# Mixer weights split once: parts kept in DRAM and loaded into the operands' ring in later blocks

## The reference

```python
z = h @ w_in                      # q, k, v, g, a_low, conv's b/c/h, cross-attention's query
o = gla_chunked(q, k, v, log_a)   # gated linear attention, 4 heads
y_gla = rms_norm(o) * silu(g)
y_conv = c_b * causal_short_conv(c_c * c_h, conv_w)
y_xa = memory_cross_attention(xq, mk, mv)           # into 256 memory tokens
mix = concatenate([y_gla, y_conv, y_xa]) @ w_out
x = layer_norm(alpha * x + mix)
ff = square(relu(x @ w_ff1)) @ w_ff2
x = layer_norm(alpha * x + ff)
```

## Time and profile before

| | us |
|---|---|
| median of 3 runs (2060.28 to 2061.87) | 2060.31 |
| the profiled execution, its own time | 2059.97 |
| its span, first to last instruction | 2058.2 |
| PE busy | 2042.5 (99%) |
| DVE busy | 1424.0 (69%) |
| ACT busy | 976.8 (47%) |
| POOL busy | 223.6 (11%) |

### The profile page before, as it was taken

One profiled execution on the slowest core, in us unless ns is written; L12 is line 12 of the kernel. 1 busy time (PEld: TensorE's weight loads), 2 busy tenths in 40 slices (PEclk: granted clock), 3 DMA queues, 4 the chain that ended last, 5 costly groups with the idle time before them and its releaser, 6 DMA issues. The chain is left out here.

```text
span 2058.2 us, 29111 instructions
## 1 busy us (share of the span) xinstructions
PE 2042.5 (99%) x11424; PEld 1679.4 (82%) x11424; DVE 1424.0 (69%) x2131; ACT 976.8 (47%) x1323; POOL 223.6 (11%) x391
## 2 busy tenths in 40 slices
PE   9999999999999999999999999999999999999998
PEld 8778788778777878888888888888888888888887
DVE  6687668756866688766757776766656668766477
ACT  5454544455445447655546544545433334433333
POOL 3000000000000003245301121111100000000000
PEclk9999999999999999999999999999999999999999
DMA  6143252425142525367566787776977657756664
GB/s 188 53 122 116 70 167 60 134 62 170 57 123 62 175 68 168 126 227 217 190 225 209 251 315 265 271 279 236 339 245 267 194 193 230 241 195 194 193 219 162
DMA packets 244329, 374.36 MB, mean 182 GB/s; under 512 B 18032, under 2 KB 119504, under 8 KB 244192
## 3 DMA queue, kind: packets, MB, share of 16 engines
q1 hardware_dynamic: 213536, 275.82, 41.4%
q0 software_dynamic: 30656, 96.67, 13.9%
HBM read 272.81 MB, written 99.61 MB: 181 GB/s over the span
## 5 line engine op out<-in xcount | busy, mean ns | idle before, releaser
L1781 DVE TENSOR_TENSOR w_lo<-w_b,w_hi 128x1024 fp32r<-128x1024 f32 x142 | 173.6, 1224 | 154.3 <-ACT w_hi L1748 154.0
L1748 ACT ACTIVATE w_hi<-raw 128x1024 fp32r<-128x1024 f32 x142 | 150.1, 1059 | 232.3 <-PE main L71 98.3
L1781 DVE TENSOR_TENSOR w_lo<-raw,w_hi 128x1024 fp32r<-128x1024 f32 x142 | 173.7, 1224 | 111.4 <-ACT w_hi L1748 111.2
L1748 ACT ACTIVATE w_hi<-w_b 128x1024 fp32r<-128x1024 f32 x142 | 150.0, 1057 | 157.5 <-PE aux L71 79.7
L69 PE MATMUL main<-xT_lo,w_hi 128*128 128x512 f32 x512 | 210.4, 411 | 0.0
L71 PE MATMUL main<-xT_hi,w_hi 128*128 128x512 f32 x512 | 200.1, 391 | 0.0
L70 PE MATMUL main<-xT_hi,w_lo 128*128 128x512 f32 x512 | 199.7, 390 | 0.0
L1137 DVE TENSOR_TENSOR w_lo<-raw,w_hi 128x1024 fp32r<-128x1024 f32 x114 | 138.8, 1221 | 70.9 <-ACT w_hi L811 69.2
L69 PE MATMUL main<-x_lo,w_hi 128*128 128x512 f32 x448 | 174.3, 389 | 0.2 <-ACT z L2092 0.2
L69 PE MATMUL sc<-x_lo,w_hi 128*128 128x512 f32 x448 | 174.3, 389 | 0.2 <-ACT z L2092 0.2
L70 PE MATMUL sc<-x_hi,w_lo 128*128 128x512 f32 x448 | 174.3, 389 | 0.0
(11 more groups left out here) (306 smaller groups left out, 4499.4 us busy)
## 6 DMA issues: line engine op xcount, KB each, us to landing
raw<-in_w_in_dram SPq DMA_DIRECT2D x80, 512.0 KB, 3.9
h_dram<-z SPq DMA_DIRECT2D x64, 512.0 KB, 4.0
raw<-h_dram SPq DMA_DIRECT2D x112, 256.0 KB, 2.7
w_b<-h_dram SPq DMA_DIRECT2D x112, 256.0 KB, 2.8
h_dram<-h_s SPq DMA_DIRECT2D x48, 512.0 KB, 4.0
raw<-in_w_out_dram SPq DMA_DIRECT2D x32, 512.0 KB, 3.5
raw<-in_w_ff_dram SPq DMA_DIRECT2D x32, 512.0 KB, 6.2
w_b<-in_w_ff_dram SPq DMA_DIRECT2D x32, 512.0 KB, 6.2
```

The lines of the kernel that those rows point to most:

```text
L1748: act.activation(hi, slot_tile(ff, m), ACT.Copy).then_inc(ff.hi_done, 1)
L1781: dve.tensor_tensor(lo, slot_tile(ff, m), hi.bitcast(F32), ALU.subtract).then_inc(ff.lo_done, 1)
```

## The change

In block 0 and in the output slots of block 1 every weight is still split, 32 splits with the four of the memory's keys and values. POOL then stores both parts to a DRAM tensor `parts_dram` (two DMAs of 512 KB a slot, 28 slots). All other slots, 20 of block 1, 28 each of blocks 2 and 3 and the eight at the end, are not split: SP loads the two stored parts straight into the ring, and PE waits for these DMAs. A split in block 0 or 1 and a load of parts wait until what was stored from the same place of the ring has landed (`saved`). The counts that the feed-forward stage waits for are shifted from `first_slot` to `first_split`.

```diff
+        slots = [(0, j) for j in range(28) if not J_OUT_B <= j < J_OUT_B + 4]
+        slots += [(t, j) for t in range(1, NBLK) for j in range(28)] + [(NBLK, j) for j in range(8)]
+        split_n, saved_n, loaded_n = {}, {}, {}
+        stores, loads = [0] * RING, [0] * RING
+        for t, j in slots:
+            saved_n[t, j] = stores[j % RING]
+            if t == 0 or t == 1 and (j < 4 or J_OUT_B <= j < J_OUT_B + 4):
+                split_n[t, j] = len(split_n)
+                stores[j % RING] += 0 if t == 0 and j < 4 else 1
+            else:
+                loads[j % RING] += 1
+                loaded_n[t, j] = loads[j % RING]
...
+        def reuse(eng, t, j):
+
+            if t == 0 and j < 16:
+                if 4 <= j < 8:
+                    eng.wait_ge(main_done, j - 3 if j < 6 else 4)
+                elif j >= 12:
+                    eng.wait_ge(main_done, slot_n(0, j - 8) + 1)
+                    eng.wait_ge(saved[j % RING], 32 * saved_n[t, j])
+                return
+            eng.wait_ge(saved[j % RING], 32 * saved_n[t, j])
...
+            def load_parts(t, j):
+                reuse(sp, t, j)
+                for i in range(2):
+                    sp.dma_start((w_hi, w_lo)[i][:, j % RING, :].bitcast(F32), parts_dram[weights_of(t, j), i, :, :]
+                                 ).then_inc(loaded[j % RING], 16)
+
             for t in range(1, NBLK):
                 for j in range(28):
-                    load(t, j, slot_source(j))
...
+                    if (t, j) in split_n:
+                        load(t, j, slot_source(j))
+                    else:
+                        load_parts(t, j)
+            for j in range(4):
+                load_parts(NBLK, j)
+            sp.wait_ge(lo_done, ff.first_split)
             sp.dma_start(w1_block(ff.w_raw[0]), w1_source(w1_v, 0, 0)).then_inc(ff.w1_landed[0], 16)
-            sp.wait_ge(lo_done, ff.first_slot)
             sp.dma_start(w1_block(ff.w_raw[1]), w1_source(w1_v, 0, 1)).then_inc(ff.w1_landed[1], 16)
+            for j in range(4, 8):
+                load_parts(NBLK, j)
...
-            pool.wait_ge(main_done, 14)
+            def store_parts(t, j):
+                pool.wait_ge(lo_done, split_n[t, j] + 1)
+                for i in range(2):
+                    pool.dma_start(parts_dram[weights_of(t, j), i, :, :], (w_hi, w_lo)[i][:, j % RING, :].bitcast(F32)
+                                   ).then_inc(saved[j % RING], 16)
+
+            for j in (4, 5, 6, 7, 12, 13, 14, 15, 16, 17):
+                store_parts(0, j)
             for j in range(4):
                 transposed(0, j)
                 load_rows(1, j, x_landed)
+            for j in range(18, 28):
+                store_parts(0, j)
+            for j in range(4):
+                store_parts(1, J_OUT_A + j)
...
+            def weights_ready(t, j):
+                if (t, j) in split_n:
+                    pe.wait_ge(lo_done, split_n[t, j] + 1)
+                else:
+                    pe.wait_ge(loaded[j % RING], 16 + 32 * loaded_n[t, j])
...
             def next_split(t, j):
 
-                split(*following(t, j))
+                if following(t, j) in split_n:
+                    split(*following(t, j))
```

More of the change, by code:

```diff
@@ L243, in hybrid_layer @@
         raw_landed = [sem(f"raw_landed{i}") for i in range(RAW)]
+        saved = [sem(f"saved{i}") for i in range(RING)]
+        loaded = [sem(f"loaded{i}") for i in range(RING)]
         hi_done, lo_done, row_used = sem("hi_done"), sem("lo_done"), sem("row_used")
@@ L255, in hybrid_layer @@
         kv_landed = [sem(f"kv_landed{i}") for i in range(2)]
-        first_landed = [sem(f"first_landed{i}") for i in range(4)]
+        first_landed = loaded
         mem_done, mem_free = sem("mem_done"), sem("mem_free")
@@ L287, in mixer_blocks_over @@
         def mixer_blocks_over(eng):
-            eng.wait_ge(lo_done, 28 * NBLK)
+            eng.wait_ge(lo_done, ff.first_split)
             eng.wait_ge(yhi_ready, 8 * NBLK)
@@ L305, in turn, with weights_of @@
             return 7 * t - 1 + j // 4
+        slots = [(0, j) for j in range(28) if not J_OUT_B <= j < J_OUT_B + 4]
[10 more added lines that the diff above has]
+                loaded_n[t, j] = loads[j % RING]
+        assert len(split_n) == ff.first_split
         def raw_turn(t, j):
-            if isinstance(t, int) and t == 0 and j < 8:
+            if t == 0 and j < 8:
                 return j // RAW if j < RAW else j // RAW - 1
-            return (4 // RAW) * (7 * t - 1) + j // RAW - 1
+            return split_n[t, j] // RAW - 1
+        def weights_of(t, j):
+            return J_OUT_B + j - 4 if t == NBLK and j >= 4 else j
+        def reuse(eng, t, j):
[7 more added lines that the diff above has]
+            eng.wait_ge(saved[j % RING], 32 * saved_n[t, j])
+            p = j - 4
+            group = {0: 0, 8: 1, 16: 2}.get(p - p % 4)
+            if t == NBLK and p >= 4:
+                group = 1
+            if p < 0 or group is None or p % 4 == 3:
+                eng.wait_ge(main_done, slot_n(t, p) + 1)
+            else:
+                eng.wait_ge(row_used, 9 * t - 6 + 3 * group + p % 4 + 1)
         def following(t, j):
@@ L341, in load @@
                 else:
-                    sp.wait_ge(lo_done, slot_n(t, j) - RAW + 1)
+                    sp.wait_ge(lo_done, split_n[t, j] - RAW + 1)
                 shape = source.shape
@@ L443, in mixer_block @@
                     load_rows(t - 1, j, res_landed)
+                if t == 1:
+                    for j in range(4):
+                        store_parts(1, J_OUT_B + j)
                 for j in range(4):
@@ L484, in column_quarter @@
                 if q == 0:
-                    pe.wait_ge(lo_done, slot_n(t, j) + 1)
+                    weights_ready(t, j)
                     pe.wait_ge(main_free[j % 4], turn(t, j))
@@ L781, in _ @@
                     x_transposes(pe, ff, X_PIECES.index(piece))
[L783 to L798, removed]
         @block.scalar
@@ L1513, in _ @@
             x_low(dve, ff, 0, 1)
-            split(NBLK, 5)
             x_sums(dve, ff, 1)
@@ L1875, in _ @@
             if chunk + 1 < CHUNKS:
-                sp.wait_ge(lo_done, FIRST + PRODUCTS * chunk + 5)
+                sp.wait_ge(lo_done, SPLITS + PRODUCTS * chunk + 5)
                 for b in range(2):
@@ L1879, in _ @@
                 for b in range(2, 4):
-                    sp.wait_ge(lo_done, FIRST + PRODUCTS * chunk + 4 + b)
+                    sp.wait_ge(lo_done, SPLITS + PRODUCTS * chunk + 4 + b)
                     sp.dma_start(w1_block(ff.w_raw[b]), w1_source(w1_v, chunk + 1, b)).then_inc(ff.w1_landed[b], 16)
@@ L2003, in expand @@
                 on = b if o in (1, 3, 5) else a
-                pe.wait_ge(lo_done, n + 1)
+                pe.wait_ge(lo_done, SPLITS + m + 1)
                 if m == 0:
@@ L2053, in contract @@
                     continue
-                pe.wait_ge(lo_done, FIRST + EXPAND_SLOTS + KF * place(hf, p) + k + 1)
+                pe.wait_ge(lo_done, SPLITS + EXPAND_SLOTS + KF * place(hf, p) + k + 1)
                 for t in range(4):
@@ L2078, in _ @@
                 if t == 0:
-                    pe.wait_ge(lo_done, FIRST + EXPAND_SLOTS + CONTRACT_SLOTS + KF * 6 + k + 1)
+                    pe.wait_ge(lo_done, SPLITS + EXPAND_SLOTS + CONTRACT_SLOTS + KF * 6 + k + 1)
                 ins = piece(1, 6, k, t)
```

24 lines of the change are left out of this document (7 added, 17 removed).

## The result

| | us |
|---|---|
| kernel before, median of 4 runs on this chip (2060.28 to 2061.87) | 2060.33 |
| changed kernel, median of 4 (2070.74 to 2074.02) | 2072.3 |
| ratio, with its 95% interval | 1.0056 (1.0039 to 1.0074) |
| changed kernel, the profiled execution's own time | 2070.74 |
| its span | 2069.0 |

The change made the kernel slower by about 12 us; the two profiled executions differ by 10.8. The forecast was 2062.5.

What follows compares the result with a forecast made beforehand. PE, 99% busy, was taken to bound the kernel. Terms -1.3 (softmax), -0.3 (mixer's end), +1.3 and +2.8 (block 0's two places) sum to +2.5 on 2059.97, giving 2062.5 us; range 2058 to 2070.

Steps and rivals of the forecast that it cites:

- What bounds the kernel, and what the splits give back: Whole kernel: PE busy 99%; 84 of 116 splits removed help only where PE waits, 3.1 us at most in the relieved stretch.
- PE's wait for the first probabilities: Softmax of blocks 2 and 3: the 0.64 us wait goes, 1.3 us gained for two times; it stays in block 1.
- The mixer's end: PE's wait for a piece of the normed rows, asked for earlier without split (4, 3): -0.3 us, bounds -0.3 and +1.6.
- The masked scores: Blocks 2 and 3: chain starts when PE's scores land and holds no split, gain 0; with the state, bounds 0 and 1.5.
- the state's waits: Relieved stretch: 1.0 us of PE's waits, in a chain that holds no split, so gain 0.
- Loads of parts hidden: Blocks 1 to 3: stored parts land before PE needs them, tightest window 16.5 us at (2, 17); cost 0, bounds 0 and 12.
- The new wait for `saved`: Block 0, ACT's split at 38.73: the stores of (0, 4) land in time for its ring place; cost 0.
- The price of a store in flight: A raw load takes 1.6 us longer for each 512 KB it stands behind, 3.2 for a slot's stores.
- Which raw loads stand behind stores: Block 0: by order of issue, only the second raw load of a pair meets the stores of the first, 3.2 us later.
- place two: Block 0, 99 to 112 us: late split at 105.33 delays masked scores and PE's attend by 2.8 us; bounds 0 and 9.
- Place one: Block 0, 27 to 54 us: late raw tile (0, 7) delays PE's transpose by 1.3 us; bounds 0 and 8.
- The second rival: Block 0: raw loads are held up by every store in flight, also ones issued after them; 2069.0 us, chance 0.27.

Runs made afterwards that it cites:

- e3: Changed kernel with only w_hi of each slot stored whole and w_lo's store cut to 8 columns, both loads reading the stored one: 2062.31 us.
- e4: Changed kernel with the same stores given out by SP on the raw loads' queue, each pair right behind the raw load its split lets go: 2066.38 us.
- e8: Changed kernel with the four row loads of block 1 put behind the stores of (0,21) instead of those of (0,17): 2073.34 us.
- e6: Changed kernel with splits in blocks 0 and 1, all stores issued in block 1 and loads of parts from block 2 on: 2064.44 us.
- e13: As e6, but stores on SP's queue two slots behind their splits, and block 2's row loads held until slot (1,20) is done: 2057.73 us.

## Why the prediction was wrong, step by step

- *What bounds the kernel, and what the splits give back*: right. PE's wait for the first probabilities went in blocks 2 and 3 and stayed in 0 and 1; each gave 0.85, not 0.64. ACT and DVE came out at 895 and 1328 us against the 888 and 1321 foreseen. The mixer's end gave 0.4, near the 0.3. The masked scores, put at nothing, gave 0.4 in each of blocks 2 and 3, for a reason that I haven't traced; the state's waits gave nothing, as said.
- *Loads of parts hidden*: right, none is waited for, and they took 3.3 and 4.4 us, the near end. *The new wait for `saved`*: no wait of PE behind it shows.
- *The price of a store in flight*, 1.6 us: right in size. e3 shows 1.4, the changed kernel 1.7 by four stores and 1.1 by six.
- *Which raw loads stand behind stores*: **wrong, and this is the step that failed.** "I take the order of issue: a raw load goes out with the store of its own pair and ahead of it, and only the second of two loads [...] meets the stores of the first." The order of issue doesn't hold between these queues. The second load stood behind four stores and more, not two (12.5 us against 5.7, 6.8 late instead of 3.2), and the next one, (0, 12), for which I counted nothing, took 9.2 against 3.8, that of (0, 14) 8.4 against 3.9. In place two it is 10.6 against 4.9, then 8.1 against 3.7. e4 shows that my rule is true where stores and loads share a queue.
- *TensorE's clock*: put at nothing without a word. About 2 us of place two are its share.
- *Place one* followed as 7.0 instead of 1.3, *place two* as 7.3 instead of 2.8. The waits were where I put them, at the transposes and the attend, but a third one came ahead of them, at the gate matmul. Place two's chain was right: its load was 5.7 us late instead of 3.2, less the 0.4 of slack makes 5.3, and the clock the rest. That e3 brings place one to 0.7 shows how narrow it was: with the two stores that I counted, its 1.3 would nearly have fitted.
- *The second rival* was the truth in its mechanism, but the sign that I gave for it, first loads that take 7 us too, is only half met. The first load of each pair took 4.4 and 5.0 us (4.0 and 4.2 before), since the stores let go with it moved their first packets some 3 us later, at 30 us and after. The loads behind the pairs, which I would have called first too, took 9.2 and 8.1. The rival's time was still too small, 2069.0 against 2070.74 of the profiled execution, because I went midway to the upper bounds of 8 and 9 (4.7 and 5.9), where PE lost 7.0 and 7.3. I left it at 0.27 although held a hint: its two loads took 10.5 and 10.2 us, and the first had only three of the four row loads issued ahead of it, for which my own rule gives 3.9 + 3 x 1.6 = 8.7. And the packets of that stretch, had I read them, show turns taken by packet where both queues had work: before, 303 to 307 us:

```profile
q0 software_dynamic: 394, 1.45, 89.5%
q1 hardware_dynamic: 324, 0.17, 13.7%
```

Packets of 3.6 KB against 0.5 KB: beside such a neighbour a raw load moves an eighth of the bytes.

## What to carry to other kernels

Before adding transfers, list for each load that something waits for what the other queues hold in flight, issued before it or after, and the packet size of each: a load of small packets beside a queue of large ones comes almost last. If it must come first, put the bulk transfers on its own queue behind it, or where no such load is due. Where one engine is busy 99% and sets the time, moving work off its neighbours is worth only its waits, here 3 us, and one collision costs more.

## What was not expected of the hardware

- Turns are taken by packet across queues, 392 packets against 354 with 1.43 MB against 0.18 MB in 4 us, while one queue keeps its order of issue (8.7 instead of 12.5 us with the same stores in flight).
- With stalls of PE of 1.9, 2.9 and 5.2 us the granted clock went to 0.50 for 3.4, 3.4 and 6.8 us; in e8's profiled execution it stayed at 1.00 after two of 3 us. The slowdown is worth 2 to 3 us of the 14; the rest of it lies ahead of another wait.
- A program's spread can change with the place of its transfers: the 11 runs of e6 span 9.4 us, those of e13 3.1. Why isn't shown.
